# A backbone of two layers: stage semaphores in two halves, and the last layer's mixing from the first latent tile

## What is computed

```python
s_lat = split_cols(h_lat @ w_in); s_ctx = split_cols(h_ctx @ w_in)
...
def bidirectional(run, ctx_fwd, lat_fwd, ctx_bwd, lat_bwd, s0, ctx_out):
    yc_f, sc_f = run(ctx_fwd, s0, ctx_out)     # context first, from the zero state
    yl_f, _ = run(lat_fwd, sc_f, True)         # latent tokens start from the context's state
    yc_b, sc_b = run(flip(ctx_bwd), s0, ctx_out)
    yl_b, _ = run(flip(lat_bwd), sc_b, True)
...
x = x + gate * (concat(branches_lat) @ w_out)
if ctx_out:                                    # false in the last layer
    ctx = ctx + gate_c * (concat(branches_ctx) @ w_out)
```

## Time and profile before

| | us |
|---|---|
| median of 3 runs (6197.98 to 6211.08) | 6207.06 |
| the profiled execution | 6209.43 |
| its span | 6207.8 |

### The profile page before, as it was taken

One profiled execution on the slowest core, in us unless ns is written; L12 is line 12 of the kernel. 1 busy time (PEld: TensorE's weight loads), 2 busy tenths in 40 slices (PEclk: granted clock), 3 DMA queues, 4 the chain that ended last, 5 costly groups with the idle time before them and its releaser, 6 DMA issues. The chain is left out here.

```text
span 6207.8 us, 76211 instructions
## 1 busy us (share of the span) xinstructions
PE 5515.7 (89%) x26532; PEld 2933.7 (47%) x26532; DVE 2911.4 (47%) x5007; ACT 1697.7 (27%) x4109; POOL 2329.4 (38%) x1718
## 2 busy tenths in 40 slices
PE   3999999967888799997979999998588877999979
PEld 1444444446666433332435454544466663333334
DVE  0354444444666555551114545455365665555312
ACT  0112111112333234444012121211133332444421
POOL 0111212123333279997001212112233332999920
PEclk7999999977999889998989999999599997999989
DMA  8223233245222100001523333333622211000032
GB/s 293 76 98 103 97 103 100 95 144 160 77 75 91 62 1 8 8 6 53 207 105 103 99 100 101 101 101 108 188 94 74 78 56 56 1 8 8 4 115 88
DMA packets 382933, 534.46 MB, mean 86 GB/s; under 512 B 114784, under 2 KB 263344, under 8 KB 375964
## 3 DMA queue, kind: packets, MB, share of 16 engines
q1 hardware_dynamic: 356124, 455.81, 22.4%
q10 hardware_dynamic: 20448, 41.46, 1.7%
q0 software_dynamic: 6048, 33.11, 1.5%
HBM read 374.82 MB, written 155.13 MB: 85 GB/s over the span
## 5 line engine op out<-in xcount | busy, mean ns | idle before, releaser
L586 PE MATMUL psum<-group_W,projection_hT 128*128 128x512 f32 (+4 forms) x5016 | 1952.7, 546 | 5.9 <-DVE projection_hT L699 5.7
L586 PEld LDWEIGHTS psum<-group_W,projection_hT 128*128 128x128 f32 x5016 | 951.1, 191 | 970.6 <-issue 929.8
L2113 POOL TENSOR_TENSOR attention_PS<-attention_PS 128x1024 f32<-128x1024 f32 x548 | 1265.6, 2354 | 82.0 <-ACT attention_PS L2246 74.7
L2159 DVE TENSOR_REDUCE attention_mxp<-psum 128x1 f32<-128x512 f32 (+1 forms) x1016 | 654.7, 686 | 541.5 <-PE psum L2295 541.5
L2246 ACT ACTIVATE attention_PS<-psum 128x512 f32<-128x512 f32 (+1 forms) x1168 | 630.6, 592 | 717.8 <-PE psum L2349 695.2
L441 POOL TENSOR_TENSOR projection_cx<-projection_cx,projection_cw 128x768 f32<-128x768 f32 x102 | 187.6, 1840 | 1686.9 <-DMA projection_cw<-in_ss_conv_w 1686.9
L2295 PE MATMUL psum<-attention_QK 32*128 32x512 f32 (+1 forms) x2592 | 771.0, 609 | 9.1 <-DVE attention_mxp L2148 6.1
L2343 PE MATMUL psum<-attention_QK 32*128 32x512 f32 x2336 | 665.1, 643 | 0.0
L2361 PE MATMUL psum<-attention_PS,attention_va 128*64 128x512 f32 x2336 | 628.1, 616 | 0.0
L650 ACT ACTIVATE projection_ut<-psum 128x256 f32<-128x256 f32 (+2 forms) x322 | 127.3, 406 | 1420.5 <-PE psum L586 1411.5
L2479 PE MATMUL psum<-output_W,output_yT 128*128 128x512 f32 x1088 | 476.9, 597 | 21.0 <-DMA output_W<-in_w_out 21.0
(11 more groups left out here) (340 smaller groups left out, 6316.4 us busy)
## 6 DMA issues: line engine op xcount, KB each, us to landing
u<-projection_ut SPq DMA_DIRECT2D x240, 256.0 KB, 2.0
projection_cx<-xbc SPq DMA_DIRECT2D x306, 128.0 KB, 2.2
projection_cw<-in_ss_conv_w SPq DMA_DIRECT2D x102, 384.0 KB, 4.6
mixing_hg<-u SPq DMA_DIRECT2D x36, 1024.0 KB, 5.1
modulation_wm<-in_w_mod SPq DMA_DIRECT2D x12, 2048.0 KB, 8.8
group_W<-in_w_in SPq DMA_DIRECT2D x8, 2316.0 KB, 34.3
output_y<-y SPq DMA_DIRECT2D x34, 512.0 KB, 4.6
group_W<-in_w_in POOLq DMA_DIRECT2D x6, 2316.0 KB, 28.9
```

The source lines that it names most:

```text
L586: ins = nc.tensor.matmul(ps[n % RING][:, lo - c0:lo - c0 + w], hT[b][:, q], W[q][:, lo:lo + w], start=(q == 0), stop=(q == KT - 1))
L2113: G.tensor_tensor(SA[x % 2][:, rs, 0:w], one[:, rs, 0:w], PT[i % PTB][:, rs, 0:w], ALU.add) \
L2159: bk.release(V.tensor_reduce(mxp[x % 2][:, q:q + nn, 2 * pr + j, a], bk[job, j][:, 0:nn * (hi - lo)].rearrange("p (q n) -> p q n", q=nn), ...
```

## The change

1. `sem` and `clear`. The semaphores of the stages come out of two fixed halves of 74 numbers each, a stage taking one half and the next stage the other. `clear` clears the stage's own range with one instruction on GpSimd and has no barrier behind it. The next stage begins right behind the closing barrier of the block.
2. `states`. In the last layer two forward steps (d = 0) over the context tiles run ahead of the 17 backward ones, so 19 steps in all. The state behind them goes to `k.st[0]`; the backward pass starts again from a tile of zeros, which both layers now set with one more memset. The last layer no longer stores the states of context tiles. In both layers the load of fi is two DMAs of 256 columns each where it was one of 512, so a step has 7 loads.
3. `mixing`. In the last layer it runs over the 16 latent tiles alone, and its first forward state is loaded from `k.st[0]` (one more DMA on SP, ahead of the first tile's loads) where a memset made it.

```diff
     def clear(self, sems):
-        for s in sems:
-            self.nc.gpsimd.sem_clear(s)
-        self.nc.all_engine_barrier()
+        assert len(list(sems)) <= self.taken
+        lo = FIRST_SEM + HALF_SEMS * self.half
+        self.nc.gpsimd.sem_clear(range(lo, lo + self.taken))
+        self.half, self.taken = 1 - self.half, 0
...
 def states(k, l):
-    d = 1
-    TILES = [*range(CT - 1, -1, -1), *range(NT - 1, CT - 1, -1)]
-    IN, RING, NLOAD = 4, 4, 6
+    ahead = CT if l == DEPTH - 1 else 0
+    BACK = [(1, t) for t in (*range(CT - 1, -1, -1), *range(NT - 1, CT - 1, -1))]
+    TILES = [(0, t) for t in range(ahead)] + BACK
+    IN, RING, NLOAD = 4, 4, 7
...
-        steps = range(NT - 1)
+        steps = range(ahead + NT - 1)
...
-                    for o, i in ((fi[b][:], u[:, OFF["hg_f"] + 256:OFF["hg_f"] + 768]),
+                    for o, i in ((fi[b][:, 0:256], u[:, OFF["hg_f"] + d * 256:OFF["hg_f"] + d * 256 + 256]),
+                                 (fi[b][:, 256:512], u[:, OFF["hg_i"]:OFF["hg_i"] + 256]),
...
+                gp.memset(zeros[:], 0.0)
                 gp.memset(S[0][:], 0.0).then_inc(s["memsets"], 1)
...
+                    if n == ahead:
+                        old = zeros
...
+                    if n < ahead or (ahead and n > ahead and TILES[n][1] < CT):
+                        act.sem_inc(s[f"st_stored{n % RING}"], 16)
+                    elif n == ahead and ahead:
+                        act.dma_start(k.st[0], S[n % RING][:]).then_inc(s[f"st_stored{n % RING}"], 16)
...
 def mixing(k, l):
+    skipped = CT if l == DEPTH - 1 else 0
+    count = NT - skipped
-    TILES = range(NT)
+    TILES = range(count)
...
                 sp.wait_ge(s["sel_in"], 16 * IN)
+                if skipped:
+                    sp.dma_start(S[0][:, 0], k.st[0]).then_inc(s["consts_in"], 16)
...
-                    gp.memset(kl[b][:], 0.0)
-                gp.memset(S[0][:, 0], 0.0).then_inc(s["pool_step"], 1)
+                    ins = gp.memset(kl[b][:], 0.0)
+                if not skipped:
+                    ins = gp.memset(S[0][:, 0], 0.0)
+                ins.then_inc(s["pool_step"], 1)
...
+                dve.wait_ge(s["consts_in"], 16 * (len(consts) + bool(skipped)))
                 for t in TILES:
...
-                pe.wait_ge(s["consts_in"], 16 * len(consts))
+                pe.wait_ge(s["consts_in"], 16 * (len(consts) + bool(skipped)))
```

More of the change, by code:

```diff
@@ L171, in sem @@
     def sem(self, c, name):
-        return c.enter_context(self.nc.semaphore(f"{self.tag}_{name}"))
+        num = None
+        if self.half is not None:
+            num = FIRST_SEM + HALF_SEMS * self.half + self.taken
+            self.taken += 1
+            assert self.taken <= HALF_SEMS
+        return c.enter_context(self.nc.semaphore(f"{self.tag}_{name}", num=num))
     def sems(self, c, names):
@@ L1128, in states @@
                       + " ".join(f"in{b}" for b in range(IN)) + " " + " ".join(f"st_stored{b}" for b in range(RING)))
-        steps = range(NT - 1)
+        steps = range(ahead + NT - 1)
+        last = len(steps)
         bk = Turns(k, c, [(("sum", n), n % 2) for n in steps] + [(("ml_hg", n), 2 + n % 2) for n in steps]
@@ L1216, in _ @@
                         update(n - 1)
-                update(NT - 2)
+                update(last - 1)
             @block.scalar
@@ L1240, in _ @@
                         store(n - 1)
-                store(NT - 2)
-                store(NT - 1)
+                store(last - 1)
+                store(last)
                 for b in range(RING):
-                    act.wait_ge(s[f"st_stored{b}"], 16 * len(range(b, NT, RING)))
+                    act.wait_ge(s[f"st_stored{b}"], 16 * len(range(b, last + 1, RING)))
             @block.tensor
@@ L1280, in _ @@
                 for n in steps:
-                    if n + 1 < NT - 1:
+                    if n + 1 < last:
                         sums(n + 1)
@@ L1301, in mixing @@
                 uses.append((("E", t, v + 2), v % 2))
-            elif t + 1 < NT:
+            elif t + 1 < count:
                 uses.append((("E", t + 1, v + 2 - STEPS), v % 2))
@@ L1316, in mixing @@
             if v == 6:
-                uses += [(("incss", t), 6)] + [(("hgT", t + 1), 4)] * (t + 1 < NT)
-    uses.append((("out", NT - 1), 4))
+                uses += [(("incss", t), 6)] + [(("hgT", t + 1), 4)] * (t + 1 < count)
+    uses.append((("out", count - 1), 4))
     with ExitStack() as c:
@@ L1500, in _ @@
                             gp.sem_inc(s["pool_done"], 1)
-                finish(NT - 1)
+                finish(count - 1)
             @block.scalar
@@ L1568, in _ @@
                             exps(t, v + 2)
-                        elif t + 1 < NT:
+                        elif t + 1 < count:
                             exps(t + 1, v + 2 - STEPS)
-                        if v == 6 and t + 1 < NT:
+                        if v == 6 and t + 1 < count:
                             turned(t + 1)
@@ L1595, in _ @@
                                 store(t - 1)
-                statistics(NT - 1)
-                store(NT - 1)
+                statistics(count - 1)
+                store(count - 1)
                 for b in range(2):
-                    act.wait_ge(s[f"y_stored{b}"], 16 * NT)
+                    act.wait_ge(s[f"y_stored{b}"], 16 * count)
             @block.vector
@@ L1754, in _ @@
                             dve.sem_inc(s["dve_done"], 1)
-                outputs(NT - 1)
-                normalise(NT - 1)
+                outputs(count - 1)
+                normalise(count - 1)
             @block.tensor
```

42 lines of the change are left out of this document (24 added, 18 removed).

## The result

| | before | after |
|---|---|---|
| median, us | 6204.52 (6197.98 to 6211.08, 4 runs) | 6109.81 (6104.64 to 6116.51, 4 runs) |
| ratio | | 0.9848 (0.9831 to 0.9865) |
| span of the profiled run, us | 6207.8 | 6106.2 |

A forecast was written before the change was run, and what follows sets the result against it. PE fills the projections and attentions, left alone, so short stages and seams were priced: -37.8 - 71.2 + 0.3 + 8.4 + 5.8 + 0.9 = -93.6 us, forecast 6114, range 6098 to 6132.

The forecast's parts named there:

- the seams: Between stages: single clears and second barrier lie on every engine's path; removing them gains 38.8 us, 37.8 net.
- the tiles that go: In mixing1: two tile intervals of 35.6 us each go, -71.2 us, bounded at 68.8 and 73.6.
- the steps that come: In the last layer's states: two more steps at 4.2 us each, +8.4 us, bounds 6.4 and 11.0.
- the loop that prices the seventh load: In states: a loop over three steps sets the pace, so each of 36 added DMAs costs 0.16 us, +5.8.
- rival 2: Between stages: clears covered something the next stage needs anyway, so none of the 37.8 us is gained: 6151; chance 0.03.
- The range clear: Between stages: one range clear costs 0.08 us like a single clear, 13 of them 1.0 us, counted on the path.
- rival 1: Between stages: a range costs as much as its members, 11.7 us less gain where GpSimd opens stages: 6125; chance 0.07.
- The start of mixing1: One more DMA on SP costs 0.9 us, less 0.6 for a memset gone: net +0.3 (-0.1 to +1.0).
- the credit of 0.6 us for the memset of S: At mixing1's opening: this memset leaves GpSimd's opening, on which DVE and then SP wait, saving 0.6 us.
- the memset: In states, both layers: one more memset ahead of SP's release, 0.5 us each, +0.9 us.
- the signs that were named: In states: line 1183 at 4.3 to 4.4 us a step; 4.7 means the issue is on the path in full.
- The rule on the fixed cost of a DMA: In states: about 2.0 us per DMA; 36 paying it on the path add 72 us, about 6180; chance 0.01.

The follow-up runs named there:

- the run with single clears: The kernel after with its range clear written out as single clears, still without the second barrier; 6122.7 us against 6207.8.
- the earlier first load: The kernel after with fi whole in backward steps, memset of zeros last layer only and behind SP's release, hg's first load ahead of SP's wait; 6098.6 us against 6206.6.
- the deeper ring: The kernel after with rings of six load buffers in states where there were four, nothing else; 6101.0 us against 6206.8.

## Why the prediction was right

All four mechanisms held: the seams, the tiles that go, the steps that come and the loop that prices the seventh load. That the two gains lie within 1.1 us of each other is partly luck, as the measurement is good to about 10 us and some terms were off in opposite directions.

**The seams.** Forecast 38.8 us, found 38.8 (the seams' sum in the table), and 40.9 by the run with the seams alone. "Every engine begins its next stage behind the same release" held; rival 2 falls with the unchanged sum of the untouched stages.

**The range clear.** The term was 13 x 0.08 = 1.0 us. It measured 3.0 in sum: two of 351, 177, 175, 285, 262 and 198 ns and one of 118. "One instruction of the same kind" was the step that failed: the duration grows by 5.5 ns a semaphore. That is rival 1 in kind but a fourteenth of it in size, and it is on the path only where GpSimd opens a stage and behind the last one, which rival 1 left out.

**Mixing1.** Forecast -71.2 with a bound of -73.6, and +0.3 at the opening. The two profiled runs differ by 74.1: the tiles' intervals by 75.0, beyond the bound, less the 0.9 of the opening. The surplus is the clock's, in this pair. Over the four profiled runs with 18 tiles mixing1 took 671.3 us on average, over the seven with 16 tiles and this opening 599.5, without the run with single clears: 71.8, where 70.9 were forecast. Two neighbouring tiles of mixing1 after, by stretch, then two of mixing1 before (columns as above; the seventh number group is the granted clock):

```profile
4525.60:4560.10 34.50, 27.46 (x243) 22.50 (x244) 21.53 (x49) 12.30 (x43) 13.03 (x16) 1.00 0.25 83
4560.10:4596.90 36.80, 30.22 (x243) 25.10 (x244) 21.72 (x49) 12.31 (x43) 13.02 (x16) 0.91 0.24 78
```

```profile
4648.40:4684.90 36.50, 30.23 (x244) 25.11 (x244) 21.61 (x49) 12.34 (x43) 13.51 (x16) 0.91 0.24 79
4684.90:4723.20 38.30, 32.11 (x244) 26.71 (x244) 21.35 (x48) 12.27 (x42) 13.03 (x16) 0.87 0.22 74
```

A tile takes 34.5 us at full clock, 36.8 at a mean of 0.91 and 38.3 at 0.87; the engine alternates between its two levels, 2.4 and 1.2 GHz, within the longer ones. Of the 16 tiles ahead of the drain before, seven were of the longer kinds, of the 14 after, five. A mean over tiles hides this. The same mixing1 of 18 tiles took 674.3, 670.6, 669.4 and 670.9 us in four profiled runs.

**The start of mixing1.** Forecast +0.3 (-0.1 to +1.0), found +0.9. The step that failed is the credit of 0.6 us for the memset of S: GpSimd's last memset was not alone in holding DVE's first cast, as the landing of a constant came as late.

**Two more steps, the seventh load and the memset.** Forecast 8.4 + 3.0 + 0.5 = 11.9 in states1 and 3.2 in states0, 15.1 in all; found 10.2 and 4.2 in the pair of profiled runs, 12.4 for both together against the run with old states. The two steps with the memset are 93.8 - 85.1 = 8.7 (fi whole, against the mean of the three stages with old states), where 8.9 were forecast. The memset is 0.5, as forecast: SP's first load in states1 goes out 1.46 us behind the release in the kernel after, and 1.00 where the memset of zeros is out of its way (the earlier first load). The seventh load was sized 0.16 us by the loop. It is 0.13 on average, and the deeper ring shows that the loop is there. What the sum did not hold is how far that price carries: at ten loads it is 0.26, since SP's own issuing sets the pace. Of the signs that were named, 4.3 to 4.4 us a step, states1 shows 4.32 and states0 4.46, slightly above and far from the 4.7 of the issue on the path in full.

**What was not forecast.** Modulation ended 4.1 us earlier, and no edit touches it. Over 12 later profiled runs, 13 with the changed kernel, it took 137.1 to 140.9 us; with the old seams alone the runs gave 137.2 (ten loads) to 141.2 (the kernel before). So this is scatter of that stage, and 4 us of the span's difference of 101.6 are not the change's. What it comes from stays open. With it taken off the spans differ by 97.5, 3.9 more than forecast, of which 3.2 is mixing1 with its clock and its opening.

**The rule on the fixed cost of a DMA.** The Trainium skill ("DMA: Bandwidth & Descriptors", anatomy of one DMA) gives its 2.0 us for DMAs that GpSimd issues, which the prediction did not say; the loads of states are SP's. As an estimate, that figure for each of the 36 DMAs would have made 72 us. The runs show 0.13 to 0.26 for one that stands in a row of others. The Trainium skill's advice to coalesce many small transfers (same title, rules for kernel authors) agrees in sign: the four added DMAs a step of the ten-load run cost 31.4 us. For the one DMA of the split alone the times show no difference.

## What to carry to other kernels

A list of instructions on one engine between two barriers costs every engine its whole length. Take away the second barrier or the list: either one alone brought four fifths of it here. To price one more DMA in a loop, look at three things in the steady part, not in the whole stage: the ring of buffers (does the queue wait for a free one), the DMA engines' share, and the queue's own issuing time. At seven loads the loop took 4.3 us a step here, the DMA engines 3.8 once the ring was deeper, and SP's issuing 7 x 0.46 = 3.2; each of them became the bound in one of the runs. Do not read the distance to the DMA engines' bound from their share alone, as the packets' time stretched from 3.8 to 4.1 us a step with the pace. When a term takes work out of one engine's opening, look at what else the next engine waits for there. Before reading a difference of a few us from two traces, lay the same untouched stages of several runs side by side.

## What the runs showed of the hardware that was not expected

- A clear of a range of semaphores on GpSimd takes 118 ns for 16, 351 for 59 and 435 for 74, while a list of single clears takes about 75 ns for each.
- The DMA engines can be filled to 0.99 of the time by loads and stores of 40 to 257 KB (290 GB/s) once the buffers are six deep; at four deep it was 0.95 at 259 GB/s, with more packet time for the same bytes.
- Ten DMA issues in a row on SP's queue take 5.0 us, 0.5 each, also when the queue waits for no buffer.
